# Shift and scale of the second layer: from TensorE row products to sums over weight rows on VectorE, ScalarE and GpSimd

## The reference, cut to what matters

```python
for i in range(DEPTH):                                   # two layers
    shift, scale, gate = jnp.split(cond @ ada_w[i] + ada_b[i], 3, axis=-1)          # tokens
    h = rmsnorm(x, norm_g[i]) * (1.0 + scale) + shift
    shift_c, scale_c, gate_c = jnp.split(cond_ctx @ ada_w[i] + ada_b[i], 3, axis=-1)  # context
    hc = rmsnorm(ctx, norm_g[i]) * (1.0 + scale_c) + shift_c
    o, oc = mixer(h, hc, ...)       # i = 0: windowed attention; i = 1: latent attention
    x = x + gate * o
    ctx = ctx + gate_c * oc
# then two more layers (pooling, dilated attention) with an MLP each
```

## Time and profile before

| what | value |
|---|---|
| runs shown | 3527.77 us median of 3, 3527.14 to 3531.81 |
| profiled execution | 3525.43 us, its span 3523.6 us |
| TensorE matmul busy | 3431.8 us, 97% of the span |
| VectorE busy | 1943.1 us, 55% |
| ScalarE busy | 1428.3 us, 41% |
| GpSimd busy | 137.8 us, 4% |
| the four panels | about 180 to 680 us of the span |

### The profile page before, as it was taken

One profiled execution on the slowest core, in us unless ns is written; L12 is line 12 of the kernel. 1 busy time (PEld: TensorE's weight loads), 2 busy tenths in 40 slices (PEclk: granted clock), 3 DMA queues, 4 the chain that ended last, 5 costly groups with the idle time before them and its releaser, 6 DMA issues.

```text
span 3523.6 us, 43632 instructions
## 1 busy us (share of the span) xinstructions
PE 3431.8 (97%) x18327; PEld 2868.5 (81%) x18327; DVE 1943.1 (55%) x2707; ACT 1428.3 (41%) x1600; POOL 137.8 (4%) x77
## 2 busy tenths in 40 slices
PE   6999999999899989999999999999999999999999
PEld 3677777777799878878888888888998788888887
DVE  2453554555668865457544554464445675445555
ACT  3223334422446543535433443353444444334432
POOL 0000000000000000005000000040000050000000
PEclk9999999999999999999999999999999999999999
DMA  8643333377332325454555555545544455555554
GB/s 339 250 157 142 132 132 120 120 255 281 124 132 101 107 106 179 167 203 175 210 196 196 185 188 190 190 175 191 179 156 156 167 191 215 191 191 191 188 194 143
DMA packets 97757, 626.07 MB, mean 178 GB/s; under 512 B 11157, under 2 KB 12182, under 8 KB 26778
## 3 DMA queue, kind: packets, MB, share of 16 engines
q1 hardware_dynamic: 92448, 606.72, 47.9%
q10 hardware_dynamic: 5114, 16.56, 1.3%
HBM read 621.14 MB, written 2.10 MB: 177 GB/s over the span
## 4 chain that ended last, share of the span: by engine, by line
PE 90%; DVE 4%; DMA 3%; ACT 2%; issue 2%; SPq 0%; DVEq 0%; ACTq 0%
PE PS L649 15%; PE PS L537 13%; PE PS L543 13%; PE PS L538 13%; PE PS L658 8%; PE PS L592 4%; PE PS L599 4%; PE PS L593 4%; DMA raw<-in_weights 3%; PE PS L673 2%; PE PS L683 2%; PE PS L829 1%; PE PS L816 1%; DVE wlo L1813 1%; PE PS L774 1%
## 5 line engine op out<-in xcount | busy, mean ns | idle before, releaser
L1813 DVE TENSOR_TENSOR wlo<-raw,whi 128x2048 fp32r<-128x2048 f32 (+1 forms) x484 | 1099.8, 2279 | 1032.6 <-ACT whi L1323 1031.7
L1323 ACT ACTIVATE whi<-raw 128x2048 fp32r<-128x2048 f32 (+1 forms) x484 | 908.7, 1885 | 1041.9 <-PE PS L543 574.9
L649 PE MATMUL PS<-xm,whi 128*128 128x512 f32 x2384 | 569.8, 391 | 0.8 <-DVE X L2296 0.8
L649 PEld LDWEIGHTS PS<-xm,whi 128*128 128x128 f32 x2384 | 438.0, 188 | 87.2 <-issue 1.6
L537 PE MATMUL PS<-whi,hid_hi 128*128 128x512 f32 x960 | 373.8, 389 | 0.0
L538 PE MATMUL PS<-whi,hid_lo 128*128 128x512 f32 x960 | 373.5, 389 | 0.0
L658 PEld LDWEIGHTS PS<-xm,wlo 128*128 128x128 f32 x2432 | 311.8, 191 | 11.9
L658 PE MATMUL PS<-xm,wlo 128*128 128x256 f32 x2432 | 315.4, 283 | 0.0
L543 PE MATMUL PS<-wlo,hid_hi 128*128 128x512 f32 x960 | 256.6, 389 | 0.0
L543 PEld LDWEIGHTS PS<-wlo,hid_hi 128*128 128x128 f32 x960 | 180.2, 188 | 37.4
L538 PEld LDWEIGHTS PS<-whi,hid_lo 128*128 128x128 f32 x960 | 180.3, 188 | 37.2
(11 more groups left out here) (382 smaller groups left out, 5361.7 us busy)
## 6 DMA issues: line engine op xcount, KB each, us to landing
raw<-in_weights SPq DMA_DIRECT2D x544, 1024.0 KB, 4.8
raw<-in_weights SPq DMA_DIRECT2D x64, 256.0 KB, 5.9
lnB<-in_ln ACTq DMA_DIRECT2D x4, 2048.0 KB, 9.2
raw<-in_weights SPq DMA_DIRECT2D x8, 768.0 KB, 4.2
X<-in_x SPq DMA_DIRECT2D x4, 1024.0 KB, 8.4
X<-in_x ACTq DMA_DIRECT2D x4, 1024.0 KB, 15.0
raw<-in_weights SPq DMA_DIRECT2D x8, 512.0 KB, 3.7
raw<-in_weights SPq DMA_DIRECT2D x4, 640.0 KB, 3.9
```

The costliest lines, as they stand in the source:

```text
L649: mm(PS[:, banks[ch // 2] + ch % 2, :], high_of(n, slice(c * PW + ch * P, c * PW + (ch + 1) * P)), x(4 * k + c).rearrange("p s t -> p (s t ...
L1323: return f(dst, src, ACT.Copy)
L1813: v.tensor_tensor(wlo[:, ring.place[n], 0:w], raw[:, ring.place[n], 0:w], whi[:, m % NH, 0:w], ALU.subtract).then_inc(lo_done, 1)
```

## The change

The tiles of `ada_w[1]` for shift and scale no longer go to TensorE. They are taken from the ring at 32 slots from block 8 of panel 0 on, 3.5 blocks apart (`ADA1_SLOT`), 20 blocks less at the end. For a tile taken in slot s:

- VectorE in slots s and s + 1 multiplies each of its four 512-column pieces with a column of `condL` (tokens) and adds it to `asum[:, :, 0]`: four instructions.
- ScalarE in slot s + 2 scales the four pieces in place with the column for the context.
- GpSimd adds the four scaled pieces to `asum[:, :, 1]` (the first piece of a group is copied).
- The place is free when GpSimd is done. TensorE's order counts it as used in slot s + 6.
- Seven slots after a group's last tile TensorE turns both sums to columns: eight matmuls of two columns against `ones`, where there were four. The copy to `arow` goes.

```diff
-ADA1_AT = {(i, 4 * j + 1): (2 * i + j // 4, j % 4) for i in range(4) for j in range(8)}
+ADA1_SLOT = [8 + 108 * m // 31 for m in range(32)]
+ADA1_AT = {divmod(s, 32): divmod(m, 4) for m, s in enumerate(ADA1_SLOT)}
+ADA1_NEXT = {divmod(s + 1, 32): divmod(m, 4) for m, s in enumerate(ADA1_SLOT)}
+ADA1_SCALED = {divmod(s + 2, 32): divmod(m, 4) for m, s in enumerate(ADA1_SLOT)}
+ADA1_USED = {divmod(s + 6, 32): divmod(m, 4) for m, s in enumerate(ADA1_SLOT)}
+ADA1_COLS = {divmod(ADA1_SLOT[4 * r + 3] + 7, 32): r for r in range(8)}
+ADA1_ADDED = {divmod(ADA1_SLOT[4 * r + 3] + 8, 32): r for r in range(8)}
...
+            def ada_sums(n, bank):
+                m = ADA1_ORDER.index(n)
+                pe.wait_ge(ada_x, 16 * (m + 1))
+                pe.wait_ge(ada_ctx, 16 * (m + 1))
+                key = ("cols", 1, n)
+                b = open_bank(key, bank)
+                for c in range(4):
+                    for s in range(2):
+                        last = mm(PS[:, b, 4 * c + 2 * s:4 * c + 2 * s + 2], asum[:, m % 2, s, c * P:(c + 1) * P], ones[:],
+                                  start=True, stop=True)
...
@@ TensorE, swa_slot
+                if (i, blk) in ADA1_USED:
+                    r, k = ADA1_USED[(i, blk)]
+                    ring.used(ada_n[r, k], (ada_ctx, 4 * (4 * r + k) + 4))
                 if (i, blk) in ADA1_AT:
                     r, k = ADA1_AT[(i, blk)]
-                    n = ADA1_ORDER[r]
-                    row_tile(("row", 1, n), ada_tiles(1, n)[k], k, 5)
-                if ADA1_AT.get((i, blk - 2), (0, 0))[1] == 3:
-                    ada_cols(1, ADA1_ORDER[ADA1_AT[(i, blk - 2)][0]], 5)
+                    ada_n[r, k] = ring.take(ada_tiles(1, ADA1_ORDER[r])[k], False)
+                if (i, blk) in ADA1_COLS:
+                    ada_sums(ADA1_ORDER[ADA1_COLS[(i, blk)]], 5)
...
@@ ScalarE, swa_slot
-                if ADA1_AT.get((i, blk), (0, 0))[1] == 3:
-                    row_kept(1, ADA1_ORDER[ADA1_AT[(i, blk)][0]])
+                if (i, blk) in ADA1_SCALED:
+                    r, k = ADA1_SCALED[(i, blk)]
+                    s = ring.place[ada_n[r, k]]
+                    for c in range(4):
+                        act.wait_ge(ada_x, 4 * (4 * r + k) + c + 1)
+                        w = raw[:, s, c * PW:(c + 1) * PW]
+                        f(w, w, ACT.Copy, scale=condL[:, 4 * k + c, 2:3]).then_inc(ada_scaled, 1)
...
@@ VectorE
+            def ada_sum(r, k, c):
+                n = 4 * r + k
+                if c == 0:
+                    s, value = ring.landed(ada_n[r, k])
+                    dve.wait_ge(landed[s], value)
+                s = ring.place[ada_n[r, k]]
+                o, w = asum[:, r % 2, 0, :], raw[:, s, c * PW:(c + 1) * PW]
+                if k == 0 and c == 0:
+                    v.tensor_scalar(o, w, condL[:, 0, 0:1], None, ALU.mult).then_inc(ada_x, 1)
+                    return
+                dve.wait_ge(ada_x, 4 * n + c)
+                v.scalar_tensor_tensor(o, w, condL[:, 4 * k + c, 0:1], o, ALU.mult, ALU.add).then_inc(ada_x, 1)
...
+                    if (i, blk) in ADA1_AT:
+                        for c in (0, 1):
+                            ada_sum(*ADA1_AT[(i, blk)], c)
+                    if (i, blk) in ADA1_NEXT:
+                        for c in (2, 3):
+                            ada_sum(*ADA1_NEXT[(i, blk)], c)
...
@@ GpSimd
+            for r in range(8):
+                if r > 1:
+                    b, v, _ = psum.at[("cols", 1, ADA1_ORDER[r - 2])]
+                    pool.wait_ge(bank_full[b], v)
+                for k in range(4):
+                    s = ring.place[ada_n[r, k]]
+                    for c in range(4):
+                        m = 4 * (4 * r + k) + c
+                        o, w = asum[:, r % 2, 1, :], raw[:, s, c * PW:(c + 1) * PW]
+                        pool.wait_ge(ada_scaled, m + 1)
+                        if k == 0 and c == 0:
+                            nc.gpsimd.tensor_copy(o, w).then_inc(ada_ctx, 1)
+                            continue
+                        pool.wait_ge(ada_ctx, m)
+                        nc.gpsimd.tensor_tensor(o, o, w, ALU.add).then_inc(ada_ctx, 1)
```

More of the change, by code:

```diff
@@ L357, in program @@
         arow = at("arow", Z + 22016, [P, PW])
+        asum = at("asum", B[5] + 8192, [P, 2, 2, PW])
         og_hi, og_lo = two("og", B[0], B[2], [P, KC, 512])
@@ L453, in program @@
         gate_clear, gate_summed = sem("gate_clear"), sem("gate_summed")
+        ada_x, ada_scaled, ada_ctx = sem("ada_x"), sem("ada_scaled"), sem("ada_ctx")
         swa_m, swa_e, swa_p, og_ready, gated = (sem(n) for n in ("swa_m", "swa_e", "swa_p", "og_ready", "gated"))
@@ L463, in program @@
         gained, mean_diag = sem("gained"), sem("mean_diag")
-        high_at, half_at, gate_n = {}, {}, {}
+        high_at, half_at, gate_n, ada_n = {}, {}, {}, {}
         block = ctx.enter_context(nc.Block())
@@ L704, in ada_cols @@
                 last.then_inc(bank_full[b], 1)
+            def ada_sums(n, bank):
[8 more added lines that the diff above has]
+                                  start=True, stop=True)
+                psum.mark(key)
+                last.then_inc(bank_full[b], 1)
             def gate_rows(s, bank, p, rows):
@@ L1403, in row_kept @@
             def row_kept(layer, n):
-                order = ADA1_ORDER if layer else [0, 4, 1] + ADA0_AT
+                order = [0, 4, 1] + ADA0_AT
                 r = order.index(n)
-                if r or layer:
-                    b, v, _ = at[("cols", layer, order[r - 1]) if r else ("cols", 0, 7)]
+                if r:
+                    b, v, _ = at[("cols", layer, order[r - 1])]
                     act.wait_ge(bank_full[b], v)
@@ L1870, in columns @@
                 b = full(key)
-                src = PS[:, b, 0:8].rearrange("p (c s) -> p s c", s=2)
+                src = (PS[:, b, 0:16].rearrange("p (c s z) -> p s c z", s=2, z=2)[:, :, :, 0] if layer
+                       else PS[:, b, 0:8].rearrange("p (c s) -> p s c", s=2))
                 bias = bcol[:, 48 * layer + 4 * n:48 * layer + 4 * n + 4].unsqueeze(1).broadcast_to([P, 2, 4])
@@ L2018, in _ @@
                         swa_step(g, n)
-                    if ADA1_AT.get((i, blk - 2), (0, 0))[1] == 3:
-                        columns(1, ADA1_ORDER[ADA1_AT[(i, blk - 2)][0]])
+                    if (i, blk) in ADA1_ADDED:
+                        columns(1, ADA1_ORDER[ADA1_ADDED[(i, blk)]])
+                    if (i, blk) in ADA1_AT:
[4 more added lines that the diff above has]
+                            ada_sum(*ADA1_NEXT[(i, blk)], c)
                     part = (HEAD_NORM_AT3 if i == 3 else HEAD_NORM_AT).get(blk)
@@ L2030, in _ @@
                     swa_step(g, n)
+                if (4, b) in ADA1_ADDED:
+                    columns(1, ADA1_ORDER[ADA1_ADDED[(4, b)]])
                 if b in OG_AT:
```

## The result

| | us | |
|---|---|---|
| before | 3527.45 | median of 4, 3527.03 to 3531.81 |
| after | 3581.88 | median of 4, 3573.86 to 3583.18 |
| ratio | 1.0146 | 95% interval 1.0135 to 1.0158 |
| forecast | 3539 | range 3503 to 3558 |

The change makes the kernel slower by 1.46%, 54 us. The direction was forecast, the size was not: the time lies 24 us above the range. The profiled execution took 3580.75 us, its span 3578.9.

What follows compares the result with a forecast made beforehand. TensorE was taken to set the time, with ScalarE and VectorE ahead of it. The profiled 3525.4 us less 28.8 saved, plus 27.5 for the ring and 13 for crowding, gave 3537.1, so 3539 us expected, range 3503 to 3558.

Steps and rivals of the forecast that it cites:

- TensorE's saving: 32 tiles leave TensorE, 38.4 us, less 9.6 for more turning to columns: its work falls by 28.8 us.
- The ring: Tiles hold three of five places longer, so loads and splits come late and TensorE waits in all panels: 27.5 us.
- Crowding: GpSimd's additions hold VectorE up beside splits and sums: 4 us each for panels 1, 2 and 3, 1 for panel 0; 13 us.
- its reserve of at least a block: Sums and scalings behind a slot's step delay the next by 2.5 us at most, which the reserve takes: zero, upper end 3 us.
- The end of panel 0: After the last split come four sums and two norms, done at T + 13.6; TensorE wants them at T + 10.9: 2.7 us.
- The clock: Rival of a lower granted clock: waits of 3.5 us in 15 could cost 3% over 100 us, 3 us; no chance given.
- VectorE the bound: Second half of panels: VectorE's busy time and waits pass TensorE's, full 1.3 us per addition: 3574 us; chance 0.15.
- the port rule of the Trainium skill: GpSimd and VectorE instructions with two SBUF inputs take one pair of ports in turn, whole instructions long; the 13 us stand without it.
- three quarters: Three quarters of the price of VectorE as the bound, given as 3556 us; it sets the range's upper end, 3558.
- The reserve holds: TensorE is two steps behind the softmax it needs, so most late splits cost nothing: 3507 us, not slower; chance 0.27.
- about even: Same chain of late splits, half of the smaller waits covered and a port that costs little: 3528 us; chance 0.18.
- the test list: Signs of being right: landing waits before nearly every split, TensorE waiting 30 to 40 us, its busy time falling by 29 us.

Runs made afterwards that it cites:

- in quarters: Changed kernel with each 512-column GpSimd addition made as four of 128 columns: 3562.2 us, ratio 1.0096.
- narrow GpSimd: GpSimd adds 8 of 512 columns in 120 of 128 additions: changed kernel 3546.4 us; changed kernel with places given back early 3513.7 us.
- the long waits: Kernel before, TensorE made to wait 8 times in panels 1 and 2 for nine GpSimd memsets: 3589.2 us, ratio 1.0170.
- the short ones: Kernel before, TensorE made to wait 24 times in panels 1 and 2 for three GpSimd memsets: 3585.9 us, ratio 1.0161.

## Why the prediction was wrong in size

- **TensorE's saving**: 28.8 forecast, 26 to 28 measured. Right.
- **The ring**: 27.5 forecast, 25 measured, and by the mechanism that it named (landing, then split, then maximum, then softmax). That the total agrees so well is in part luck: some 10 of the 25 us are TensorE's longer busy time at the lower clock (3410.0 against 3400.3), which the term did not have, so the waits are some 15 us where 27.5 were worked out. GpSimd's releases, which I counted at nothing, held the loads up 70.3 us; in quarters it was 135.5 and the kernel got faster, and with a narrow GpSimd the gain was no larger where it frees places (36 us) than where it frees none (42), so they were of little weight.
- **Crowding: the step that failed.** The prediction has "half of each addition's 1.3 us holds VectorE up", and that was about right: VectorE was busy for 87.6 us longer than with a narrow GpSimd (2115.9 against 2028.3), 0.73 us for each of 120 additions. What failed is what followed, "4 us for each of the panels". TensorE felt 36 to 42 us of it. I weighed VectorE's busy time against the length of half a panel, and there it still had room: from 355 to 425 us, the second half of panel 1, it was busy 58.86 of 70. But it works in order, and what TensorE needs next (the last product of a norm, a maximum, `Sb`) stood behind sums, splits and small operations that were each held up by an addition. In the short stretches in front of TensorE's waits VectorE was full: 42.57 of 44 us at the end of panel 0 (240 to 284), 10.48 of 11 in front of the wait of 3.73 us. The average over half a panel hides them. Twelve us more came from the sums and scalings as such, priced at nothing because of "its reserve of at least a block".
- **The end of panel 0**: 2.7 us forecast for the norms, 12.44 measured, by the same stretching: with a narrow GpSimd none of the three waits for a last norm is over 2.4 us.
- **The clock**: 3 us forecast as a rival inside the range, from one window; TensorE's busy time says 32.8. It comes with the waits: by the medians each us of waiting brought some 0.3 to 0.4 us more with it in the runs with waits put in (18 on 42.4, 14 on 43.4), by the traces 24.9 on 42.4 and 16.1 on 43.4. In the kernel after it was 31.3 on 49.8, 0.63 on one, close to the 0.59 of the long waits; why it is nearer to those than to the short ones stays open. Every term of a sum made of TensorE's waits must carry this.
- **The rivals**: "VectorE the bound" came nearest with 3574 at its full price, and it had the port rule of the Trainium skill behind it, with a chance of 0.15. Its condition (work and waits beyond TensorE's time in a stretch) was met in the second half of panel 0 from 240 us on (42.57 of 44 us, TensorE 31.21) and in short stretches of panel 1, not over the whole second half of panel 1, for which the prediction counted it; nor was the full 1.3 us of an addition lost each time (0.73). So its number came near by a partly different way. Its "three quarters", 3556, are a slip: three quarters of 35 us on 3539 are 3565. The range's upper end of 3558 rests on that number; with 3565 the time would still lie above it. "The reserve holds" and "about even" did not happen.

In the test list, the landing waits and the waits for `Sb` and bank 6 came, fewer than written: 16 landing waits, not one before nearly every split, and 20.0 us of TensorE for `Sb` and bank 6 together, not 30 to 40. The load of the split at 396.15 us went out at 391.23, 0.2 us behind the last product of the block before. TensorE's busy time did not fall by 29 us, and the windows grew. Two of the signs of being wrong came too: SyncE waited last for GpSimd's `ada_ctx` (21 times), and sums that waited for additions filled VectorE for the last 44 us of panel 0, if not for a whole panel.

## What to carry to other kernels

Price work that is moved to another engine by what stands behind it in that queue and by when TensorE needs that, not by the engine's busy share over a long stretch, and each new wait of TensorE at 1.3 to 1.6 times its length. Keep long GpSimd additions away from a VectorE that feeds TensorE (giving VectorE their work as well, with the places free sooner, was 51 us cheaper), or make them short. Spread moved work thinly: half of the tiles at half the density cost about 19 us where all cost 80.

## What the runs showed of the hardware

- A GpSimd addition of 512 columns took 1.52 us in the mean beside VectorE, each of four of 128 columns 0.63: shorter instructions cost GpSimd 56% more time in all (285.4 us against 182.4) and gave the kernel 20 us.
- VectorE's operations of 128x16 took 0.17 us. In the kernel after, the four of `hrs<-nt` took 0.93 in the mean and the twelve two-input ones of `nt<-nt,hrs` 0.43, one by one either 0.17 or about 1.2; with memsets of 0.53 us beside them it was 485 and 175 ns.
- After one wait of 5.3 us TensorE's granted clock was 0.51 for some 6 us, then 1.00.
